# A two-layer hybrid trunk: the mixers normalise probabilities before they are transposed and move them wide over stationary values, and the second mixer's local branch works on chunks of 128 tokens

## The chip, the cores and the metric

The kernel is one program on 1 core of one Trainium2 chip. The metric is the device time in microseconds of that core. It was run 3 times before the change.

## The reference

A trunk of two layers on x of 512 tokens by 1024 channels, in float32. Each layer is a half-weighted SwiGLU, a mixer, and another SwiGLU, each with an RMS norm that is shifted and scaled by a projection of the condition c. Between the two layers one shared set of keys and values for three branches is projected. The mixers are what the change touches:

```python
# first mixer (MoBA): with 512 tokens and blocks of 256 its selection keeps every past block: causal attention
p = jax.nn.softmax(jnp.concatenate([s_own, s_sel], axis=-1), axis=-1)
# second mixer: branches (window, dilation) = (128, 1), (512, 4), (2048, 16), each a band of 128 strided keys or fewer
m = jnp.max(s, axis=-1, keepdims=True)
p = jnp.exp(s - m)
l = jnp.sum(p, axis=-1, keepdims=True)
o = jnp.einsum('nbhqk,nbkhd->nbqhd', (p / l), v_band)
lse = (m + jnp.log(l))[..., 0]
...
w = jax.nn.softmax(jnp.stack(lses, axis=0), axis=0)
o = jnp.einsum('gbsh,gbshd->bshd', w, jnp.stack(outs, axis=0))
return o.reshape(B, S, ATTN_DIM) @ w_o
```

Both mixers have 16 heads of 64 channels. In the second, weighting the branches by the softmax of their lse is the same as one softmax over the keys of all three.

## The kernel before, in words

All activations lie transposed (channels on the 128 partitions, 512 tokens along the free axis). Float32 accuracy comes from splitting: every operand x is held as a rounded high part and a low part of the type float32r, and a product is three matmuls, hi x hi, lo x hi, hi x lo (`three_passes`, lines 344 to 347). ScalarE makes the high part (line 336), VectorE (DVE) the low one (line 340). Weights stream through two slots of 512 KB (`w_dma`, line 326), read once.

The program's order is: four SwiGLU blocks (ffn0 to ffn3) with mixA between the first two, the shared k/v projection (kv) after ffn1, and mixB between ffn2 and ffn3. Each engine has its order written out; semaphores join them. GpSimd (POOL) does only the rotary additions (lines 1456 and 1462), a few low parts and the stores; SyncE (SP) issues all loads.

A mixer (`pe_mixer`, line 670, with `act_mixer`, `dve_mixer`, `pool_mixer` and `sp_mixer` for the other engines) works in 4 groups g of 4 heads. While group g is projected (24 substeps of 6 matmuls of 512 columns, or 12 of 256 for the values of mixA), the attention of group a = g - 1 runs; the last attention group runs beside the output projection. An attention group has 16 steps, one for each head and each tile of 128 queries. In step s TensorE does, in this order:

- `score`: queries stationary, keys moving. In mixA the past keys, 128 to 512 columns. In mixB the tokens lie sorted by their class modulo 4; the local branch scores all 512 keys under a mask, the two dilated ones 128 each, so 768 columns. Each part is a pair of matmuls, keys high and keys low.
- one or two projection substeps (table `SUBSTEPS`, line 98), or parts of the output projection in the last group (`OUT_SUBSTEPS`, lines 119 to 121, steps 1 to 14).
- `transpose_p`: the step before's probabilities, 1 to 4 or 6 transposes of 128x128.
- `weigh_v`: of two steps before; probabilities stationary, high and low, the values of the head moving (2 x 64 columns, high and low), 2 matmuls for each 128 keys.

Between these, DVE takes the masked minimum of the negated scores in one operation (line 1973), ScalarE the exponential with its row sum (line 1796), ScalarE and DVE split the transposed probabilities (lines 1803 and 1996), and DVE adds the two halves of the output, inverts the row sum and scales (`o_scale`, lines 1981 to 1990). After two heads `transpose_o` turns the output's rows into columns.

Rotated queries and keys go to DRAM and come back per head (`load_k`, `load_q`, `load_v`, lines 1655 to 1710): 8 loads of keys and 4 of queries, each to 32 partitions, of 192 KB in mixB and 64 KB in mixA, and one load of values. They have two slots, so a head's loads are held until the head before has begun:

```python
sp.wait_ge(done, (a * 4 + (0 if layer == "A" else HEADS) + j - 1) * 4 + 1)   # head_free, line 1657
```

In mixB the third branch's queries skip DRAM at a group's end (line 1681): read out at step 14 (`READ_OUT`, line 108), added by POOL, split by ScalarE and DVE, then sent on. SP works through its list in order: keys, queries, values, weight units.

Of the kernel before, what the change touches and what calls it, by code (L numbers as in the profile page):

```python
# [32 lines left out]
P = 128  # L33
# [88 lines left out]
OUT_HIGH = {0: 2, 1: 3, 3: 4, 5: 5, 7: 6, 8: 7, 12: 8, 15: 9}  # L122
OUT_LOW = {1: 2, 2: 3, 4: 4, 6: 5, 8: 6, 9: 7, 13: 8}
OUT_ADD = {1: 0, 2: 1, 4: 2, 5: 3, 7: 4, 9: 5, 12: 6}
OUT_IN = {13: (6,)}
POOL_ROWS = (0, 1, 2, 3, 4, 6)


OUT_BY_POOL = 5
OUT_IN_AHEAD = {"mixA": {10: (0,), 11: (1,), 12: (2,), 13: (3,), 14: (4,)}, "mixB": {11: (0, 1), 12: (2, 3), 13: (4,)}}  # L130
TAIL_BANK = {"woA": (0, 1, 2, 3, 4, 6, 5, 0), "woB": (0, 1, 2, 4, 5, 6, 7, 0)}
# [16 lines left out]
def build(nc, x_t, c_col, ada_first, ada, ada_bias, gains, gate_up, down, mixa_w, kv_w, mixb_w, cos_t, sin_t,  # L148
          mask_a, mask_b, ident_in, out):
    with ExitStack() as ctx:  # L150
# [47 lines left out]
        with ExitStack() as mixer_space:  # L198
# [9 lines left out]
            probs = sb(mixer_space, "probs", [P, 2, 6 * P])  # L208
            pt_hi = sb(mixer_space, "pt_hi", [P, 2, 6 * P], F32R)
            pt_lo = sb(mixer_space, "pt_lo", [P, 2, 6 * P], F32R)  # L210
            o_rows = sb(mixer_space, "o_rows", [P, TT, 4 * HD])
            att = sb(mixer_space, "att", [P, KT, S])
            m_a = sb(mixer_space, "m_a", [P, TT * P], BF16)
            m_b = sb(mixer_space, "m_b", [P, TT, 6 * P], BF16)
            negmax = sb(mixer_space, "negmax", [P, 2])
            denom = sb(mixer_space, "denom", [P, 4])
            rdenom = sb(mixer_space, "rdenom", [P, 2])
# [11 lines left out]
        scores = flat[:, 4 * 512:4 * 512 + 6 * P]  # L229
        pt_ps = flat[:, 6 * 512:6 * 512 + 6 * P]  # L230
        O_BANK = {"A": 5, "B": 3}
        OT_BANK = {"A": 7, "B": 3}
        V_BANK = 4

# [40 lines left out]
        q_landed, k_landed, v_landed = sem("q_landed"), sem("k_landed"), sem("v_landed")  # L275
# [3 lines left out]
        s_done, negmax_done, exp_done = sem("s_done"), sem("negmax_done"), sem("exp_done")  # L279
        t_done, pt_hi_done, pt_lo_done = sem("t_done"), sem("pt_hi_done"), sem("pt_lo_done")  # L280
        pv_done, rd_done, o_done = sem("pv_done"), sem("rd_done"), sem("o_done")
        o_sum_done = sem("o_sum_done")
        ot_done = sem("ot_done")
        att_done = sem("att_done")
# [2135 lines left out]
```

## Time and profile before

| what | value |
|---|---|
| median of 3 runs | 2465.88 us (2465.1 to 2468.98) |
| profiled execution, its span | 2469.2 us, within 0.1% of the slowest of the three runs |
| PE busy | 2432.8 us, 99% |
| DVE busy | 1378.1 us, 56% |
| ScalarE busy | 867.2 us, 35% |
| POOL busy | 143.2 us, 6% |
| moved by DMA | 408.8 MB, mean 166 GB/s |

Engine names in the rows: PE is TensorE, PEld its weight loads, DVE VectorE, ACT ScalarE, POOL GpSimd, SPq the DMA issues of SyncE. A line of the timeline gives start, duration, engine, source line, operation, output <- inputs, and in brackets the idle time before it. The duration of a matmul includes its way through the array, and the next one starts before it ends; what one costs is the distance to the next one's start. PEclk is the granted share of TensorE's full clock. The DMA share is the mean busy share of the 16 DMA engines in a stretch. mixA's attention lies between 457 and 680 us, mixB's between 1751 and 2080 us.

### The profile page before, as it was taken

How to read it: one execution, taken by the hardware profiler on the slowest of the kernel's cores; microseconds unless marked ns; L12 is line 12 of the kernel's file. 1: busy time of each engine (PE TensorE's matmuls, PEld its weight loads, DVE VectorE, ACT ScalarE, POOL GpSimd, SP SyncE). 2: the span in 40 equal slices, each digit the busy share in tenths (PEclk: the TensorE clock that was granted, in tenths of full speed). 3: DMA queues.
4: the chain of work that ended last, by engine and by line, in shares of the span. 5: the costliest groups of instructions: out<-in, count | busy, mean ns of one | idle time of the engine just before them, and what ended most of it. 6: DMA issues, size and time to landing. Idle time of an engine off the chain costs nothing. (4 is left out here: it accounts for less than half of the span.)

```text
span 2469.2 us, 33249 instructions
## 1 busy us (share of the span) xinstructions
PE 2432.8 (99%) x11992; PEld 2022.7 (82%) x11997; DVE 1378.1 (56%) x2103; ACT 867.2 (35%) x1233; POOL 143.2 (6%) x130
## 2 busy tenths in 40 slices
PE   9999999999999999999999999999999999999998
PEld 6888888888778888888888888888888887888886
DVE  7555546777675654465545555446667667333333
ACT  3322224445343332233333333223444444333221
POOL 0000000212000000011211000000211100000000
PEclk9999999999999999999999999999999999999999
DMA  6665543665446654336557656436878973222332
GB/s 246 192 194 188 167 126 92 214 192 179 143 154 194 188 181 138 103 114 214 185 189 246 191 182 196 132 119 166 245 218 224 240 214 93 94 93 93 102 94 85
DMA packets 135779, 408.80 MB, mean 166 GB/s; under 512 B 17152, under 2 KB 17536, under 8 KB 135680
## 3 DMA queue, kind: packets, MB, share of 16 engines
q1 hardware_dynamic: 122624, 357.16, 47.8%
q0 software_dynamic: 13056, 50.33, 5.7%
q8 instruction: 60, 0.98, 0.2%
q14 instruction: 39, 0.32, 0.0%
HBM read 353.42 MB, written 52.43 MB: 164 GB/s over the span
## 5 line engine op out<-in xcount | busy, mean ns | idle before, releaser
L340 DVE TENSOR_TENSOR w_lo<-w_raw,w_hi 128x1024 fp32r<-128x1024 f32 (+2 forms) x386 | 473.9, 1228 | 605.4 <-ACT w_hi L336 605.1
L345 PE MATMUL ps<-h_hi,w_hi 128*128 128x512 f32 x1872 | 744.7, 398 | 5.9 <-DVE w_lo L340 2.7
L347 PE MATMUL ps<-h_hi,w_lo 128*128 128x512 f32 x1872 | 731.6, 391 | 0.0
L346 PE MATMUL ps<-h_lo,w_hi 128*128 128x512 f32 x1872 | 730.9, 390 | 0.0
L336 ACT CAST w_hi<-w_raw 128x1024 fp32r<-128x1024 f32 (+2 forms) x388 | 395.6, 1020 | 757.8 <-PE ps L347 737.1
L345 PEld LDWEIGHTS ps<-h_hi,w_hi 128*128 128x128 f32 x1872 | 352.8, 188 | 81.5 <-DVE w_lo L340 5.3
L347 PEld LDWEIGHTS ps<-h_hi,w_lo 128*128 128x128 f32 x1872 | 352.3, 188 | 74.9
L346 PEld LDWEIGHTS ps<-h_lo,w_hi 128*128 128x128 f32 x1872 | 353.0, 189 | 66.9 <-issue 0.2
L345 PE MATMUL ps<-act_hi,w_hi 128*128 128x512 f32 x704 | 275.3, 391 | 0.3 <-DVE w_lo L340 0.2
L347 PE MATMUL ps<-act_hi,w_lo 128*128 128x512 f32 x704 | 274.1, 389 | 0.0
L346 PE MATMUL ps<-act_lo,w_hi 128*128 128x512 f32 x704 | 273.9, 389 | 0.0
L1334 DVE TENSOR_TENSOR prod<-ps,silu_g 128x512 f32<-128x512 f32 x86 | 59.5, 692 | 259.2 <-ACT silu_g L1292 259.2
L892 DVE SCALAR_TENSOR_TENSOR ada_acc<-ada_raw,c_act,ada_acc 128x1024 f32<-128x1024 f32 x126 | 161.2, 1279 | 0.7
L345 PEld LDWEIGHTS ps<-act_hi,w_hi 128*128 128x128 f32 x704 | 132.1, 188 | 31.3 <-issue 4.3
L347 PEld LDWEIGHTS ps<-act_hi,w_lo 128*128 128x128 f32 x704 | 132.1, 188 | 27.9
L346 PEld LDWEIGHTS ps<-act_lo,w_hi 128*128 128x128 f32 x704 | 132.2, 188 | 27.1
L1803 ACT CAST pt_hi<-ps 128x768 fp32r<-128x768 f32 (+4 forms) x128 | 78.4, 612 | 215.4 <-PE ps L754 215.2
L1292 ACT ACTIVATE silu_g<-ps 128x512 f32<-128x512 f32 x86 | 51.5, 599 | 252.3 <-PE ps L347 252.0
L1996 DVE TENSOR_TENSOR pt_lo<-ps,pt_hi 128x768 fp32r<-128x768 f32 (+4 forms) x128 | 92.4, 722 | 80.7 <-ACT pt_hi L1803 79.8
L773 PE MATMUL ps<-v_st,pt_hi 128*128 128x128 f32 x544 | 129.8, 278 | 4.6 <-DVE o_rows L1990 4.6
L774 PE MATMUL ps<-v_st,pt_lo 128*128 128x128 f32 x544 | 128.1, 275 | 0.0
L1456 POOL TENSOR_TENSOR rotated<-tmp 128x512 f32<-128x512 f32 x32 | 43.5, 1359 | 1425.6 <-DVE tmp L1023 1233.4
(162 smaller groups left out, 2802.6 us busy)
## 6 DMA issues: line engine op xcount, KB each, us to landing
w_raw<-gate_up SPq DMA_DIRECT2D x176, 512.0 KB, 3.7
ada_raw<-ada SPq DMA_DIRECT2D x144, 512.0 KB, 4.5
w_raw<-down SPq DMA_DIRECT2D x80, 512.0 KB, 3.6
w_raw<-kv_w SPq DMA_DIRECT2D x48, 512.0 KB, 3.5
w_raw<-mixa_w SPq DMA_DIRECT2D x34, 512.0 KB, 3.9
w_raw<-mixb_w SPq DMA_DIRECT2D x34, 512.0 KB, 5.9
kb<-rot_st POOLq DMA_DIRECT2D x12, 1024.0 KB, 5.0
k_hi<-kb SPq DMA_DIRECT2D x64, 192.0 KB, 5.0
```

The costliest lines, as they stand in the source:

```text
L336: nc.scalar.copy(w_hi[:, slot, 0:n], w_raw[:, slot, 0:n]).then_inc(w_hi_done, 1)
L340: eng.tensor_tensor(w_lo[:, slot, 0:n], w_raw[:, slot, 0:n], w_hi[:, slot, 0:n].bitcast(F32), ALU.subtract).then_inc(w_lo_done[slot], 2)
L345: nc.tensor.matmul(out_ap, l_hi, r_hi, start=start, stop=False, skip_group_check=skip)
L346: nc.tensor.matmul(out_ap, l_hi, r_lo, start=False, stop=False, skip_group_check=skip)
L347: return nc.tensor.matmul(out_ap, l_lo, r_hi, start=False, stop=stop, skip_group_check=skip)
L773: nc.tensor.matmul(o_ps, pt_hi[:, s % 2, cols], v_both, start=n == 0, stop=False)
L774: mm = nc.tensor.matmul(o_ps, pt_lo[:, s % 2, cols], v_both, start=False, stop=n == n_last)
L892: nc.vector.scalar_tensor_tensor(out=ada_acc[:], in0=ada_raw[:, slot, :], scalar=c_act[:, k:k + 1], in1=ada_acc[:], op0=ALU.mult, op1=ALU. ...
L1292: nc.scalar.activation(silu_g[:, b, :], ps[:, 2 * b, :], ACT.Silu).then_inc(silu_done, 1)
L1334: nc.vector.tensor_tensor(prod[:, b, :], ps[:, 2 * b + 1, :], silu_g[:, b, :], ALU.mult).then_inc(pair_free, 1)
L1803: nc.scalar.copy(pt_hi[:, s % 2, 0:w], pt_ps[:, 0:w]).then_inc(pt_hi_done, 1)
L1996: nc.vector.tensor_tensor(pt_lo[:, s % 2, 0:w], pt_ps[:, 0:w], pt_hi[:, s % 2, 0:w].bitcast(F32), ALU.subtract).then_inc(pt_lo_done, 1)
```

## The change

Both mixers: the row sum is inverted right after the exponential, POOL multiplies the probabilities by it, and they are transposed and split already normalised. `weigh_v` now runs once per head: values are stationary (their high half and low half side by side give 128 output rows), the normalised probabilities of up to four query tiles move over them, and the output comes out transposed. `transpose_o` goes; ScalarE copies one half (`fold_copy`), DVE adds the other (`fold_add`). Transposes run 2 steps (mixA) or 5 steps (mixB) behind the scores.

mixB: the local branch takes queries and keys in token order, in chunks of 128, each chunk against itself and the one before: 128 or 256 columns instead of 512. The dilated branches stay sorted by class. So a row of local scores and a row of dilated scores belong to different tokens; minimum and sum are kept per branch kind, exchanged by one small matmul per head (`exchange`, `lanes`), and the joint factor is built by ten small DVE operations and one exponential, once per head, before POOL scales that head's four steps. The rotary additions write the local branch in chunk order. The values of the local branch are loaded by 4 DMAs to 32 partitions each.

```diff
-OUT_SUBSTEPS = {1: [(0, (5,)), (1, (5,))]}
-OUT_SUBSTEPS |= {step: OUT_PARTS[2 * step - 4:2 * step - 2] for step in range(2, 7)}
-OUT_SUBSTEPS |= {step: OUT_PARTS[step + 3:step + 4] for step in range(7, 15)}
+LAG = {"A": 2, "B": 5}
+SLOTS = {"A": 4, "B": 6}
+OUT_SUBSTEPS = {
+    "A": {4: OUT_LAST} | {step: OUT_PARTS[2 * step - 10:2 * step - 8] for step in range(5, 10)}
+    | {step: OUT_PARTS[step:step + 1] for step in range(10, 18)},
+    "B": {7: OUT_LAST} | {step: OUT_PARTS[step - 8:step - 7] for step in range(8, 16)}
+    | {step: OUT_PARTS[2 * step - 24:2 * step - 22] for step in range(16, 21)}}
...
+                if st >= 2:
+                    pe.wait_ge(negmax_done["B"], 2 * st - 2)
+                q, past = q_st[:, sl, 0, tile], slice(max(i - 1, 0) * P, (i + 1) * P)
+                kh, kl = k_hi[:, sl, 0, past], k_lo[:, sl, 0, past]
...
+            def exchange(h):
+                pe.wait_ge(spread_ready, 2 * h + 2)
+                nc.tensor.matmul(spread_ps, lanes[:, 0:P], spread_in[:].rearrange("p s e x y -> p (s e x y)"),
+                                 start=True, stop=True).then_inc(spread_done, 1)
...
+            def weigh_v(h):
...
+                if is_a:
+                    for n in range(TT):
+                        for pt in (pt_hi, pt_lo):
+                            mm = nc.tensor.matmul(o[:, n * P:], v(0, n), pt[:, n, n:4, :].rearrange("p i q -> p (i q)"),
...
+                by_chunk = o.rearrange("p (t c l) -> p t c l", t=4, c=4)
+                for c in range(4):
+                    for b in (1, 2):
+                        for pt in (pt_hi, pt_lo):
+                            nc.tensor.matmul(by_chunk[:, :, c, :], v(b, c),
+                                             pt[:, c, 1 + b, :].rearrange("p (t l) -> p t l", t=4),
...
+            def begin(st, first=(), second=()):
+                if st < ROWS:
+                    score(st)
+                for part in first:
+                    part()
+                if not is_a and st % 4 == 0 and 4 <= st <= ROWS:
+                    exchange(st // 4 - 1)
+                if (st - lag) % 4 == 0 and st - lag >= 4:
+                    weigh_v((st - lag) // 4 - 1)
+                for part in second:
+                    part()
+                if 0 <= st - lag < ROWS:
+                    transpose_p(st - lag)
...
+            for c in range(4):
+                sp.dma_start(v_st[32 * c:32 * c + 32, j % 2, 0].rearrange("p t a d -> p t (a d)").bitcast(F32),
+                             dram_v["B"][a, 0, j].rearrange("(u l) (t n) -> l u t n", l=32, t=4)[:, :, c, :]
+                             ).then_inc(v_landed[j % 2], 16)
...
+                for e, cols in enumerate((slice(P if i == 0 else 0, 2 * P), slice(2 * P, 4 * P))):
+                    op = nc.gpsimd.tensor_scalar(slot[:, cols], slot[:, cols], factor_b[:, h % 2, e, i:i + 1], 1.0,
+                                                 ALU.mult, ALU.mult)
```

Two places where the order of instructions matters. On SP, in a group of mixB with projections, one head's loads (k_hi, k_lo, q_st, v_st are the slots of keys, queries and values; kb, qb, vb the tensors in DRAM; w_raw a weight slot). Before:

```order
L1644 DMA k_hi<-kb 32x3x512 x2
L1644 DMA k_lo<-kb 32x3x512 x2
L1644 DMA k_hi<-kb 32x3x512 x2
L1644 DMA k_lo<-kb 32x3x512 x2
L1644 DMA q_st<-qb 32x3x512 x4
L1672 DMA v_st<-vb 128x3x512
```

and now:

```order
L1678 DMA k_hi<-kb 32x3x512 x2
L1678 DMA k_lo<-kb 32x3x512 x2
L1678 DMA k_hi<-kb 32x3x512 x2
L1678 DMA k_lo<-kb 32x3x512 x2
L1678 DMA q_st<-qb 32x3x512 x4
L1719 DMA v_st<-vb 32x4x128 x4
L1722 DMA v_st<-vb 128x2x512
```

Keys and queries are loaded as before; the values (of the head before that one now) take five DMAs instead of one, four of them of 32 partitions.

On PE, in the last attention group of mixB, one early step that isn't a head's first (probs are the probabilities before the transposes, pt_hi and pt_lo after, ps is the accumulator). Before, step 5:

```order
L744 MATMUL ps<-k_hi,q_st 128x512
L745 MATMUL ps<-k_lo,q_st 128x512
L744 MATMUL ps<-k_hi,q_st 128x128
L745 MATMUL ps<-k_lo,q_st 128x128
L744 MATMUL ps<-k_hi,q_st 128x128
L745 MATMUL ps<-k_lo,q_st 128x128
L345 MATMUL ps<-h_hi,w_hi 128x512
L346 MATMUL ps<-h_lo,w_hi 128x512
L347 MATMUL ps<-h_hi,w_lo 128x512
```

and now the whole step:

```order
L776 MATMUL ps<-k_hi,q_st 128x256
L777 MATMUL ps<-k_lo,q_st 128x256
L780 MATMUL ps<-k_hi,q_st 128x128
L781 MATMUL ps<-k_lo,q_st 128x128
L780 MATMUL ps<-k_hi,q_st 128x128
L781 MATMUL ps<-k_lo,q_st 128x128
L796 MATMUL ps<-ident,probs 128x128 x4
```

The local pair is 256 columns wide, the parts of the output projection behind the score have moved to steps 7 to 20, and the value products stand once per head.

## Rows read from the trace of the kernel before

**Rows 1.** The page: the span, and part 1's first engine.
```profile
span 2469.2 us, 33249 instructions
...
PE 2432.8 (99%) x11992; PEld 2022.7 (82%) x11997; DVE 1378.1 (56%) x2103; ACT 867.2 (35%) x1233; POOL 143.2 (6%) x130
```
**Rows 2.** Windows view: mixB's attention groups two to four.
```profile
core 0: us, PE busy (x) PEld busy (x) DVE busy (x) ACT busy (x) POOL busy (x), PEclk, DMA share, GB/s
...
1828.30:1911.60 83.30, 81.53 (x538) 72.30 (x538) 57.13 (x117) 37.66 (x59) 9.88 (x9) 1.00 0.85 230
1911.60:1993.80 82.20, 80.19 (x531) 71.09 (x530) 55.45 (x117) 38.66 (x63) 16.18 (x14) 1.00 0.88 226
1993.80:2082.70 88.90, 86.39 (x556) 75.53 (x556) 57.62 (x122) 39.59 (x66) 3.67 (x2) 1.00 0.62 166
```
**Rows 3.** Timeline view of PE in mixA: start us, duration us, then the matmul.
```profile
577.37 0.45 PE L744 MATMUL ps<-k_hi,q_st 128*128 128x512 f32 x1
...
577.89 0.39 PE L345 MATMUL ps<-h_hi,w_hi 128*128 128x512 f32 x1
578.11 0.39 PE L346 MATMUL ps<-h_lo,w_hi 128*128 128x512 f32 x1
...
581.14 0.27 PE L773 MATMUL ps<-v_st,pt_hi 128*128 128x128 f32 x1
581.26 0.27 PE L774 MATMUL ps<-v_st,pt_lo 128*128 128x128 f32 x1
...
583.03 0.60 PE L754 MATMUL ps<-ident,probs 128*128 128x128 f32 x4
583.39 0.31 PE L773 MATMUL ps<-v_st,pt_hi 128*128 128x128 f32 x1
...
584.09 0.33 PE L744 MATMUL ps<-k_hi,q_st 128*128 128x256 f32 x1
...
584.38 0.39 PE L345 MATMUL ps<-h_hi,w_hi 128*128 128x512 f32 x1
```
**Rows 4.** Timeline view of SP's DMA issues: first key loads of head 10 in mixB.
```profile
1932.97 1.58 SPq L1644 DMA_DIRECT2D k_hi<-kb  x2
```
**Rows 5.** Tile view of q_st: the same head's query loads, last of its twelve.
```profile
L1644 SPq DMA_DIRECT2D q_st<-qb x4: 317/365/373, 1938.0 to 1939.4; - x4
...
DMA to landing us min/median/max: 5.6/6.1/6.6
```
**Rows 6.** Timeline view of PE: first scores of heads 9 and 10 in mixB.
```profile
1931.69 0.48 PE L744 MATMUL ps<-k_hi,q_st 128*128 128x512 f32 x1 [0.74 <-issue]
...
1948.89 0.45 PE L744 MATMUL ps<-k_hi,q_st 128*128 128x512 f32 x1
```
**Rows 7.** Windows view: a stretch of key and query loads, one of weight and value loads.
```profile
1787.00:1795.00 8.00, 8.00 (x59) 7.31 (x58) 5.35 (x13) 3.89 (x6) 1.06 (x1) 1.00 1.06 219
...
1782.00:1784.50 2.50, 2.50 (x16) 2.11 (x16) 2.39 (x7) 0.63 (x2) 0.00 (x0) 1.00 1.06 419
```
**Rows 8.** Timeline view at a group's end: step 14, read-out, rotation, low part, DMAs, next score.
```profile
1891.90 0.45 PE L744 MATMUL ps<-k_hi,q_st 128*128 128x512 f32 x1
...
1896.72 0.68 DVE L1440 TENSOR_TENSOR tmp<-ps,sin 128x512 f32<-128x512 f32 x1
...
1898.72 1.27 POOL L1462 TENSOR_TENSOR rotated<-tmp 128x512 f32<-128x512 f32 x1
...
1902.52 1.21 DVE L1480 TENSOR_TENSOR rot_st<-rotated,rot_st 128x1024 fp32r<-128x1024 f32 x1
...
1903.76 2.70 SPq L1681 DMA_DIRECT2D q_st<-rot_st  x4
...
1911.57 0.39 PE L744 MATMUL ps<-k_hi,q_st 128*128 128x512 f32 x1
```
**Rows 9.** Windows view at the end of mixA's third group: before and in a clock drop.
```profile
614.00:618.00 4.00, 2.55 (x16) 1.82 (x15) 3.53 (x10) 1.35 (x4) 2.43 (x2) 1.00 0.62 148
618.00:621.40 3.40, 3.40 (x10) 2.62 (x9) 0.35 (x2) 0.00 (x0) 0.00 (x0) 0.50 0.96 345
```

More of the change, by code:

```diff
@@ L1607, in pool_kv @@
             body(0, True)
-            with pool.Fori(1, G * NB // 2) as i:
+            for i in range(1, G * NB // 2):
                 body(i)
@@ L1756, in sp_mixer @@
[L1756 to L1768 removed]
+                        unit(g, 5)
@@ new lines, in sp_mixer, with out_unit, loads @@
+            group = group_a if layer == "A" else group_b
+            group(0, None)
+            for g in range(1, G):
+                group(g, g - 1)
+            a = G - 1
+            def out_unit(n):
+                w_dma(sp, u0 + n, n % 2, weights[n])
+            def loads(j):
+                load_k(sp, layer, a, j)
+                load_q(sp, layer, a, j)
+            if layer == "A":
+                loads(1)
+                load_v(sp, "A", a, 1)
+                loads(2)
+                out_unit(28)
+                out_unit(29)
+                load_v(sp, "A", a, 2)
+                out_unit(30)
+                out_unit(31)
+                loads(3)
+                out_unit(32)
+                load_v(sp, "A", a, 3)
+                out_unit(33)
+                return
@@ new lines, in begin, with add @@
+            def begin(st):
+                if is_a and 1 <= st <= ROWS:
+                    scale(st - 1)
+                if not is_a and st % 4 == 1 and 5 <= st <= ROWS + 1:
+                    for i in range(4):
+                        scale(st - 5 + i)
+            def add(g, pair):
+                n = g * (2 if is_a else 3) + rope0 // 2 + pair
+                first = g == 0
+                rope_add(pool, g * 3 + p0 + pair, n, name if pair == 0 and first else None,
+                         (1 if is_a else 1 + pair) if pair > 0 and first else None, chunks=not is_a and pair == 0)
@@ new lines, in pool_mixer @@
+            for pair in range(3):
+                if not (is_a and pair == 2):
+                    add(0, pair)
+                store(0, pair)
+            if is_a:
+                pool.wait_ge(k_landed, 128)
+                rot_store(pool, rope0 // 2 + 1, dram_q["A"][0, 0], q_stored)
+            adds = {2: 0, 8: 1} if is_a else {2: 0, 8: 1, 14: 2}
+            stores = {5: 0, 11: 1, 15: 2}
+            for g in range(1, G):
+                for s in range(STEPS):
+                    begin((g - 1) * STEPS + s)
+                    if s in adds:
+                        add(g, adds[s])
+                    if g == G - 1:
+                        for k in POOL_IN_AHEAD[name].get(s, ()):
+                            pool_out_in(pool, wo, k)
+                    if s in stores:
+                        store(g, stores[s])
@@ L2146, in build @@
+            for s in range(STEPS + lag + 1):
+                if s == POOL_LAST[layer]:
+                    pool_out_in(pool, wo, POOL_ROWS[-1])
+                begin((G - 1) * STEPS + s)
+            w_split_lo(pool, UNIT0[wo] + 9, 1)
         block = ctx.enter_context(nc.Block())
```

765 lines of the change are left out of this document (404 added, 361 removed).

## The prediction

> **What bounds the kernel now.** I read the page first: TensorE (PE) is busy for 2432.8 of 2469.2 us [rows 1], so time comes out only where PE's own work shrinks, and only as far as nothing else then makes PE wait. The windows view of three attention groups of the second mixer comes next [rows 2]: 83.3, 82.2 and 88.9 us each, PE busy for 97%, VectorE (DVE) for 57 of 83 us, but the 16 DMA engines for 0.85 and 0.88. That last column is what the prediction turns on. The PE timeline [rows 3] gives what a matmul costs, as the distance between starts (the durations overlap): a 512-column one 0.22 (577.89 to 578.11), a 128-column one 0.12 in the printed rows and 0.11 over longer runs of them, a pair of 128 some 0.22, a score pair of 512 columns 0.52, a pair of 256 0.29, four transposes 0.36 to 0.40, 0.10 each. The counts below are the code's.
>
> **PE work, first mixer.** A head's value products are 20 of 128 columns (rows of probabilities stationary); they become 2 each of 512, 384, 256 and 128 (values stationary). 20 x 0.11 = 2.2 us becomes 2 x (0.23 + 0.17 + 0.12 + 0.11) = 1.27; 384 and 256 alone are put between the 128 and the 512 by columns. The 2 transposes of the output per head (0.2) go. 1.15 us less for each of 16 heads: 18.
>
> **PE work, second mixer**, per head. Scores: 4 x (0.52 + 2 x 0.22) = 3.84 becomes, with 128 or 256 local columns, 0.66 + 3 x 0.73 = 2.85. Transposes: 24 become 15, 2.4 to 1.5. Value products: 48 of 128 columns, 5.3, become 18 of 128 and 6 of 256, 2.7. Output transposes: 0.2 go. Added: one matmul of 64 columns in plain f32, which no row has in that width; between a pair of 128 columns (0.22) and one of 512 (0.52) I take 0.25, as it is narrower than the first. 11.8 becomes 7.3, so 4.5 x 16 = 72 us. **PE work falls by 90 us.** The k/v stage only orders rotated columns otherwise on GpSimd, whose cover is the whole stage's matmuls: 0.
>
> **Other engines.** DVE loses the row sum and scaling per step (three short ones) and halves the columns of its largest two; it gains a second minimum, some ten tiny operations and one 512-column add per head. It stays near 58 us of a group, under PE's 66. GpSimd now multiplies every probability: 1920 columns per head. Its two-input operation takes 1.27 us for 512 [rows 8], so 4.7 us per head at most, beside a head window of 13; the lag of five steps holds it. It waits in program order behind its rotations (2.5 us), also inside the lag. I cost both at 0, and they are in the upper part of the range.
>
> **What then waits: the loads of the second mixer.** A head's keys and queries come in 12 DMAs of 192 KB to 32 partitions each, and SyncE may send them only once the first score of the head before has run. Head 10: first score of head 9 at 1931.69 [rows 6], first K load 1932.97 [rows 4], last Q load issued at 1939.4 and landed 6.6 later at most [rows 5], so 14.3 us after that score; head 10's first score ran at 1948.89 [rows 6]. **The slack was 2.9 us of 17.2.** The chain can't shrink: such loads run at 219 GB/s with all 16 engines occupied (share 1.06; packets overlap), where weights run at 419 at the same share [rows 7]; 2.36 MB / 219 = 10.8 us. The change doesn't touch them. It does change the values' load: the local 256 KB now also go to 32 partitions in pieces of 512 bytes. At 219 instead of 419 that is 1.2 instead of 0.6 us; nothing shorter than 2 KB is in this stage, so the upper end is twice that.
> Windows of PE work per head afterwards, in a group with projections (one projection step is 6 x 0.23 = 1.4):
> - heads 0 and 3: 7.3 + 8 x 1.4 = 18.5. Head 0 covers the 14.3 of the next head's loads.
> - heads 1 and 2: 7.3 + 4 x 1.4 = 12.9, with change-overs between kinds 13.3. DMA time per head is 10.8 (keys, queries), 2.5 (values), 1.3 (one weight unit) and 1.9 (three quarters of a 1 MB store at 419) = 16.5. Two heads in a row: the second set of loads lands some 30.7 us after head 1's first score (3 to start, 10.8, 6.1 of the others, 10.8), PE's work is 26.6: 4 us of waiting per group.
> - group end: the queries of the next group go through DVE, GpSimd, ScalarE, DVE and a DMA [rows 8]. Step 14's score, to which the read-outs are tied, stood at 1891.90, the last DMA was issued by 1906.46, and I add 1.2 for its landing (64 KB, nothing in front): 15.8 us. PE's work in that time was 19.7 (next score at 1911.57) and is now step 14 (1.1), step 15 (2.6) and five projection steps (6.9), 10.6. 4.5 to 5 us of waiting at each of 3 group ends.
> - last group: the output-projection parts move from steps 1 to 14 to steps 7 to 20, so steps 0 to 6 hold attention alone. Windows 7.3, 8.7 and 12.9 against 14.3: 7 + 5.6 + 1.5 = 14 us.
> In sum 3 x 8.5 + 14 = 40 us. The first mixer's loads are a third of the size; 12 issues take 6.8 us (1932.97 to 1939.8) [rows 4, 5] and some 2 to land, against 10 or more of PE work in a head, except in the last group, where four steps without parts hold 4 to 5: 4 us.
> **The clock.** PE ran at half clock for 3.4 us (granted 0.50, 1.2 instead of 2.4 GHz) after a stretch of 4 us in which it was busy for 2.55 [rows 9]. Waits of 5 us are such stretches. Where PE is then the bound (three group ends) each costs half of 3.4: 5 us; in the last group the next loads cover it. The Trainium skill (TensorE: Matmul & The Clock Gate, Part 1) has the half clock as the default that activity releases, so it would add as much behind every long wait.
>
> **Sum**: 2469.2 - 90 + 40 + 4 + 5 = 2428 for the profiled span. The median of the runs lies 3.3 below that span: 2425. Ends of the unknown costs: waits of 20 (engines interleave the loads better, the query chain shortens with DVE's load) to 70 (512-byte pieces at the dear end, stores that fall in front of keys, GpSimd late).
>
> **Rivals.**
> - *All waits covered*: PE stays the only bound: 2466 - 90 + 5 to 25 = 2381 to 2401. For it: DMA share was 0.85, not 1. Against: the same DMA time, 0.85 x 83 = 71 us per group, doesn't fit in 83 - 18 = 65. 16%.
> - *DMA bound with gaps*: a group can't run under 71 + 3 for the values, plus idle DMA time whenever SyncE stands at a semaphore (now a tenth of the group): 80 us per group, so the second mixer gains only in its last group; with clock losses 2445 to 2460. 16%.
> - *The column order costs the matmuls*: 16 of a head's 24 value products write four runs of 32 columns each, spread over a whole bank. All 128-column rows here write one run. If a write of the bank's full spread costs as a 512-column one, 0.23 instead of 0.11, 256 x 0.12 = 30 us come back: 2455, 4%. **It decides the sign** from 0.11 + 41/256 = 0.27 us each; at 0.45 (double a 512-column one) it adds 87, 2512: slower. The Trainium skill (SBUF — State Buffer, Door 1, its note on cache lines) says that any non-contiguous access to PSUM slows matmuls much. For it: the rule names no shortest run; against: runs of 32 f32 are contiguous over far more than one such line. 5%.
> - That the change doesn't do what it says I rule out by the order of its instructions: the counts above are read there.
>
> **Chances.** Forecast (waits of 30 to 65 us, 2405 to 2445) 58%; covered 16%; DMA bound 16%; column order, part 4%, slower 5%; all cancelled, 1%. 0.2% (5 us) is what a measurement of this kernel tells from no change. Faster 0.93, same 0.02, slower 0.05. The range leaves out half of the covered case and the slower one: 2393 to 2455.
>
> **What would show it.** PE busy down by about 90 us and its idle time up by 35 to 50, nearly all of it before the first score of a head and ended by the landing of keys or queries; group periods near 68, 74, 73 and 85 us; DMA share in the groups at 0.95 or more; more stretches of granted clock 0.5. Wrong if value products stand further apart than 0.12, if PE waits mainly for scaled probabilities (GpSimd) or for DVE, or if the DMA share stays under 0.9 while PE still waits.

## The result and the profile after

| | median of the runs | ratio to before, 95% interval |
|---|---|---|
| before | 2467.1 us (4 runs, beside those of the change) | |
| after | 2505.9 us (2503.8 to 2512.6, 4 runs) | 1.0161, 1.0146 to 1.0176 |

Slower by 39 us where 41 us faster was forecast. The profiled execution, whose span of 2510.8 us is used below, is the longest of the four; the spans of the others are 2502.0 to 2505.2. The page of the changed kernel, its span, the engines and, in 40 slices, the granted clock of TensorE (PE):

```profile
span 2510.8 us, 31515 instructions
...
PE 2393.7 (95%) x11245; PEld 1972.4 (79%) x11245; DVE 1325.9 (53%) x2087; ACT 875.2 (35%) x1397; POOL 250.1 (10%) x322
...
PEclk9999999999899999999999999999999879999999
```

Against [rows 1] PE is busy 39 us less, not 90, although the products forecast away are away. It also stands idle for 117 us, not 36. The windows view cuts the two mixers into their first three attention groups and the rest (last group up to the norm behind it). Before:

```profile
core 0: us, PE busy (x) PEld busy (x) DVE busy (x) ACT busy (x) POOL busy (x), PEclk, DMA share, GB/s
457.60:624.80 167.20, 161.67 (x1039) 142.69 (x1040) 116.85 (x342) 79.79 (x184) 30.78 (x27) 0.99 0.63 199
624.80:692.30 67.50, 63.03 (x340) 49.96 (x339) 46.76 (x129) 31.08 (x70) 3.90 (x2) 1.00 0.36 112
1751.00:1993.80 242.80, 237.50 (x1578) 211.03 (x1579) 166.93 (x347) 113.85 (x181) 36.73 (x33) 1.00 0.84 224
1993.80:2087.20 93.40, 89.98 (x571) 76.97 (x570) 61.97 (x129) 42.41 (x70) 3.67 (x2) 1.00 0.59 158
```

After, the same four stretches:

```profile
456.90:628.30 171.40, 151.35 (x856) 127.58 (x857) 95.62 (x254) 83.99 (x187) 65.12 (x74) 0.97 0.63 192
628.30:713.10 84.80, 68.49 (x299) 52.69 (x297) 44.83 (x105) 36.56 (x76) 13.09 (x19) 0.88 0.32 94
1770.20:2010.70 240.50, 197.36 (x1115) 167.86 (x1113) 140.83 (x403) 107.73 (x287) 79.85 (x120) 0.91 0.88 223
2010.70:2128.80 118.10, 98.48 (x509) 83.49 (x509) 59.24 (x169) 46.78 (x117) 23.40 (x43) 0.83 0.55 132
```

Three things stand in these rows. The loss lies in the two last groups: 67.5 to 84.8 us and 93.4 to 118.1, together +42. The three groups with projections are 4.2 longer in mixA and 2.3 shorter in mixB, though PE's work there fell by some 63 us (the table below). And the clock, 0.99 to 1.00 before, is 0.97, 0.88, 0.91 and 0.83.

To part these I took every distance between two matmul starts of both traces. The lower quartile of a kind of pair at full clock is its **work**; of what a distance has above it, the part inside a stretch of granted clock 0.5, up to once the work, is **half clock**, the rest **waits**:

| us | length | work | half clock | waits |
|---|---|---|---|---|
| mixA, groups 1 to 3 | 167.2 to 171.4 | 149.6 to 140.1 | 1.6 to 4.7 | 16.9 to 27.2 |
| mixA, last group | 67.5 to 84.8 | 58.9 to 57.4 | 0 to 7.9 | 9.0 to 19.6 |
| mixB, groups 1 to 3 | 242.8 to 240.5 | 225.1 to 171.3 | 0 to 17.1 | 18.6 to 53.6 |
| mixB, last group | 93.4 to 118.1 | 85.4 to 80.4 | 0 to 16.9 | 8.5 to 21.3 |
| change | +44 | -70 | +45 | +69 |

The three parts of a row add up to its length within 1.5 us. They depend on which pairs count as one kind: told apart by tiles and widths alone, single entries move by up to 5 us and the sums read -68, +44 and +68. Outside the mixers the changed kernel is 2 us shorter. **Waits and half clock give back 114 us for 70.** The waits view of PE names the waits in mixB (us in total, times, longest; DVE is VectorE, and pt_lo the low part of the split transposed probabilities):

```profile
PE ps L776 <- DMA q_st<-rot_st: 13.7, 3, 4.8
PE ps L821 <- DVE pt_lo L2123: 11.4, 9, 3.0
PE ps L796 <- DVE pt_lo L2123: 10.8, 12, 1.4
PE ps L787 <- DVE spread_in L2088: 8.8, 7, 2.4
PE ps L776 <- issue: 8.6, 5, 3.3
```

L776 are a head's first scores, L821 value products, L796 transposes, L787 the exchange. The first and the last row (22 us) stand before a head's first scores, where the forecast had put its waits for queries and keys; the trace names no releaser for the last, and run 11 shows that it was the loads. The three between (31 us, all ended by DVE) were not forecast. In mixA:

```profile
PE ps L812 <- DVE pt_lo L2123: 10.8, 11, 2.8
PE ps L796 <- DVE pt_lo L2123: 10.3, 16, 1.9
PE ps L765 <- DVE negmax L2062: 5.9, 14, 1.3
```

Before, the largest such row in either mixer was 3.2 us. Now one exchange and what follows, from the timeline (start us, duration us):

```profile
1896.06 1.22 DVE L1513 TENSOR_TENSOR rot_st<-rotated,rot_st 128x1024 fp32r<-128x1024 f32 x1
1897.19 0.28 DVE L2062 CUSTOM_DVE_ANT_0 probs<-ps,m_b 128x128 f32<-128x128 f32 x1
...
1897.75 0.29 DVE L2088 TENSOR_TENSOR spread_in<-stats,lanes 128x32 f32<-128x32 f32 x2
...
1898.09 0.43 PE L787 MATMUL ps<-spread_in,lanes 128*128 128x64 f32 x2 [1.78 <-DVE spread_in L2088]
...
1899.76 0.73 PE L377 MATMUL ps<-h_hi,w_hi 128*128 128x512 f32 x1
1900.20 0.69 DVE L2123 TENSOR_TENSOR pt_lo<-ps,pt_hi 128x512 fp32r<-128x512 f32 x1 [0.75 <-ACT pt_hi L1903]
1900.29 0.63 PE L378 MATMUL ps<-h_lo,w_hi 128*128 128x512 f32 x1
1900.71 0.63 PE L379 MATMUL ps<-h_hi,w_lo 128*128 128x512 f32 x1
...
1901.51 3.54 POOL L2259 TENSOR_SCALAR probs<-probs,factor_b 128x128 f32<-128x128 f32 x8 [2.84 <-DVE factor_b L2115]
...
1902.42 0.26 PE L821 MATMUL ps<-pt_hi,v_st 128*128 128x128 f32 x1
...
1905.13 0.52 PE L796 MATMUL ps<-ident,probs 128*128 128x128 f32 x3
```

DVE's queue has a rotation's split of 1.2 us ahead of what the exchange needs; PE stands 1.78 us at L787. The transposes that PE began at 1898.36 were split by 1900.89, 2.5 us later; in between ScalarE had stood 0.97 us for the exchange's result before it could round them. Behind it the projection matmuls are 0.42 to 0.53 apart in place of 0.23: the clock fell at 1899.1, for 3.4 us. The 24 value products take 1902.42 to 1905.13, 2.7 us, as forecast.

The clock also stays low in stretches where PE doesn't wait. Windows of the last group of mixB, steps 0 to 6, in which no output part stands:

```profile
2010.70:2016.00 5.30, 3.70 (x19) 3.38 (x19) 2.51 (x13) 1.67 (x6) 0.81 (x1) 0.60 0.68 219
2016.00:2021.00 5.00, 5.00 (x24) 5.00 (x25) 1.03 (x6) 1.09 (x4) 3.54 (x8) 0.50 1.05 243
...
2027.00:2033.00 6.00, 4.46 (x19) 4.12 (x20) 3.27 (x14) 2.28 (x9) 0.00 (x0) 0.50 0.83 206
2033.00:2039.00 6.00, 6.00 (x29) 6.00 (x30) 1.18 (x6) 1.83 (x6) 3.54 (x8) 0.50 1.03 226
```

### The profile page after: what moved, and what is told of

It is laid out like the page before. It is cut to its first block and busy times, and to the rows that moved or that the text cites. A ratio compares the mean times of both kernels' runs of the same rounds, so it can differ in the third digit from the quotient of the medians.

```text
span 2510.8 us, 31515 instructions
## 1 busy us (share of the span) xinstructions
PE 2393.7 (95%) x11245; PEld 1972.4 (79%) x11245; DVE 1325.9 (53%) x2087; ACT 875.2 (35%) x1397; POOL 250.1 (10%) x322
## 5 line engine op out<-in xcount | busy, mean ns | idle before, releaser
L377 PE MATMUL ps<-h_hi,w_hi 128*128 128x512 f32 x1872 | 749.5, 400 | 18.9 <-DVE w_lo L372 6.2
L377 PEld LDWEIGHTS ps<-h_hi,w_hi 128*128 128x128 f32 x1872 | 356.9, 191 | 95.1 <-DVE w_lo L372 11.1
L377 PE MATMUL ps<-act_hi,w_hi 128*128 128x512 f32 x704 | 275.3, 391 | 0.0
L377 PEld LDWEIGHTS ps<-act_hi,w_hi 128*128 128x128 f32 x704 | 132.1, 188 | 31.0 <-issue 3.9
L2123 DVE TENSOR_TENSOR pt_lo<-ps,pt_hi 128x512 fp32r<-128x512 f32 (+3 forms) x128 | 73.2, 572 | 129.7 <-ACT pt_hi L1903 128.4
L1888 ACT ACTIVATE probs<-probs,stats 128x256 f32<-128x256 f32 (+1 forms) x128 | 62.4, 488 | 116.0 <-DVE stats L2062 115.9
L796 PE MATMUL ps<-ident,probs 128*128 128x128 f32 x400 | 71.5, 293 | 21.0 <-DVE pt_lo L2123 21.0
```

The costliest lines, as they stand in the source:

```text
L377: nc.tensor.matmul(out_ap, l_hi, r_hi, start=start, stop=False, skip_group_check=skip)
L796: mm = nc.tensor.transpose(pt_ps[:, n, :], probs[:, st % SLOTS[layer], n * P:(n + 1) * P], ident[:])
L1888: nc.scalar.activation(slot[:, cols], slot[:, cols], ACT.Exp, bias=stats[:, h % 2, 0, e, i:i + 1], scale=-1.0, accum_out=stats[:, h % 2, 1 ...
L2123: nc.vector.tensor_tensor(lo, src, hi.bitcast(F32), ALU.subtract).then_inc(pt_lo_done[layer], 1)
```

## The experiments

In the order in which they ran; the kernel before was run beside each set of them (medians 2466.2 to 2469.1). The changed kernel, 2505.9, is the reference unless another is named.

**1. Fillers before known waits.**
```diff
+ nc.tensor.matmul(ps[:, 3, 64:], idle[:, 0:P], idle[:, 64:], start=True, stop=True)
+ FILL_HEAD, FILL_SPREAD, FILL_WEIGH = (14, 2, 5, 0), (1, 1, 6, 1), (3, 2, 0, 3)   # how many, by h % 4
```


> Some 150 matmuls on a tile of zeros (0.2 us each at full clock, 29 us in all) stand in the second mixer where the trace of the changed kernel shows TensorE waiting: ahead of the first scores of a head, of the exchange and of the value products. Their results are never read. Theory C (the waits are what drops the clock to 0.5, and the half clock costs by itself some 32 us in this mixer beside the waits): the granted clock there rises from 0.73-0.92 to 0.97 or more, the fillers lie inside waits, and the kernel is 15 to 25 us faster than the changed kernel, 2481 to 2491. Rival L (the waits are latency and transfers; at full clock TensorE would only wait longer for them): the clock rises too, the time stays within 5 us of 2506. Rival W (the fillers are work like any other): 2520 to 2535.

2511.8 us (1.0169, 1.0148 to 1.0189). In mixB waits fell by 14 us, work rose by 15, half clock went from 34 to 31. Theory C fell: zeros ahead of the waits did not bring the clock back, and the time came out a little above what rival L allows. Whether waits alone set the clock is left open by this.

**2. Loads one step earlier.**
```diff
-  if h >= (1 if layer == "A" else 2): sp.wait_ge(s_done[layer], 4 * (h - 1) + 1)
+  if h >= 2: sp.wait_ge(s_done[layer], 4 * (h - 1))     # k_landed, q_landed: one semaphore per slot
```


> The keys and queries of a head are sent for when the last scores of the head two before are done, not one step later, after the first scores of the head before (the landings are counted on two semaphores in turn, for the order). Theory L (TensorE's waits before the first scores of a head, 24 us in the second mixer, are the transfer's, and it starts a step too late): the waits for the second to fourth heads of a group (some 10 us) go, those at a group's start (4.7 us each, the query chain) stay, a few clock drops go with them: 2490 to 2500. Rival D (DMA queues full, share 0.85 to 0.94 there: sent earlier, not landed earlier): 2503 to 2508.

2506.9 us (1.0155, 1.0134 to 1.0177): level. Rival D's result: the waits of 8.6 us before other heads' first scores read 8.3.

**3. The exchange at its step's end** (PE, ACT and DVE alike).
```diff
+  if 0 <= st - lag < ROWS: transpose_p(st - lag)     # DVE: split_pt, then find_gap and joint_factor
   if not is_a and st % 4 == 0 and 4 <= st <= ROWS: exchange(st // 4 - 1)
-  if 0 <= st - lag < ROWS: transpose_p(st - lag)
```


> Second mixer: the exchange across the groups of 32 partitions and what DVE and ACT do with it stand at the end of their step, behind the transposes, their rounding and their splitting. Theory X (TensorE waits 7 us for the exchange's operand and DVE, standing in the exchange, holds up the split that the value products one step on wait for, 11 us): 8 to 15 us faster than the changed kernel, 2491 to 2498. Rival F (the factors then come late and the transposes of the next step wait for POOL's scaled rows instead): 2500 to 2515, with a new row of TensorE waiting for scaled probabilities.

2493.9 us (1.0100, 1.0083 to 1.0117): 12 us of the 39 by the medians (14 when each is set against the runs of the kernel before beside it), as theory X had it, and the largest single gain of the study. The waits of PE in mixB now:

```profile
PE ps L796 <- DVE pt_lo L2123: 17.9, 16, 2.0
PE ps L776 <- DMA q_st<-rot_st: 12.2, 3, 4.7
PE ps L776 <- issue: 11.3, 7, 2.5
...
PE ps L787 <- DVE spread_in L2088: 2.7, 5, 1.2
...
PE ps L821 <- DVE pt_lo L2123: 0.7, 1, 0.7
```

The exchange went from 8.8 to 2.7 and the value products from 11.4 to 0.7, but the transposes from 10.8 to 17.9: a part of the repaired wait opened one step on.

**4. No scaling by POOL.**
```diff
-  pe.wait_ge(scaled_done[layer], st + 1)
+  pe.wait_ge(exp_done[layer], st + 1 if is_a else 2 * st + 2)
```


> Both mixers: POOL scales nothing, and the transposes wait for the exponentials alone; the probabilities go on unscaled (this part of the computation is left out). Theory N (normalising first puts factor and scaling into the chain, and the lags of 2 and 5 steps don't cover it): 15 to 30 us faster, 2476 to 2491, and the waits of TensorE for pt_lo fall by half. Rival S (the scaling is covered by the lags; the waits are the turn of the one PSUM bank of the transposes through ACT and DVE): 2500 to 2506, waits as they were.

2505.6 us (1.0148, 1.0130 to 1.0165). POOL's busy time fell from 250 to 146 us and the time stayed: rival S. PE's waits for pt_lo in mixB read 8.8 and 10.8 us, for 11.4 and 10.8. As it stands the change doesn't lose by the scaling.

**5. Projection parts ahead of a group's first scores** (on run 3).
```diff
-  pre = FIRST_PRE[layer] if g == 1 else PRE
+  pre = FIRST_PRE[layer] if g == 1 or not is_a else PRE        # 10 in place of 6; SUBSTEPS likewise
```


> On top of the late exchange (2493.9): in the second mixer four gemm parts (1.4 us each) move from the first four steps of a group ahead of the group's first scores, where TensorE waits 4.7 us for the landing of the last query block. Theory Q (that wait is latency, and work put there is free; the steps they leave get short, but not shorter than the 14.3 us in which the next head's keys and queries come): the three waits of 4.7 us go, with them the clock drop behind each: 12 to 20 us faster than 2493.9, 2474 to 2482. Rival M (the parts are missing in the first head: its steps wait for the landing of the second head and for the turn of the transposes' bank instead): 2490 to 2500.

2491.6 us (1.0094, 1.0078 to 1.0111): within the noise of run 3. Two of three waits for the query block went, and a new one of 3.8 us each took their place (`PE ps L377 <- DVE tmp L1468: 7.6, 2, 3.8`, the read-out of the bank of a later part). Rival M's time by another wait than it named.

**6. A part for step 14 of mixA** (on run 3).
```diff
+  steps = {step: steps.get(step, ())[:1] if step == 3 else steps.get(step, ()) for step in range(4)} \
+      | {step: (step + 9,) for step in range(4, 15)}
```


> On top of the late exchange: in the first mixer the gemm parts of steps 3 to 13 are shifted by one, so that step 14, which had none, has one (step 3 has one in place of two). Theory G (the value products of step 14 wait 1.6 to 2.3 us for the split just before them because no part lies between): these three waits and the two clock drops behind them go, 5 to 9 us faster than 2493.9. Rival H (every part taken out of one step opens the same wait in another): 2491 to 2497.

2516.6 us (1.0197, 1.0180 to 1.0214), 23 us slower than run 3, which neither theory had. The first three groups of mixA became 190.7 us in place of 170.7, and the value products of nine of their twelve heads now waited 2.2 to 3.2 us for pt_lo. PE's table was shifted and those of ACT and DVE (weight splits, read-outs) were not. That their queues then stand at a part that comes a step later, with the split of the probabilities behind it, fits; it was not tried with all tables shifted.

**7. Two banks for mixA's transposes** (on run 3).
```diff
+  def pt_bank(layer, st): return ps[:, 7 if layer == "A" and st % 2 == 1 else 6, :]
-  return ps[:, 5 if layer == "B" or h % 2 == 0 else 7, :]
+  return ps[:, 5, :]
```


> On top of the late exchange: in the first mixer the transposes take banks 6 and 7 in turn and the value products one bank in place of two, so that transposes wait for the split of the tile two back. Theory B (TensorE waits 10 us there for the turn of the one bank): these waits fall below 3 us, with them a clock drop or two: 8 to 14 us faster than 2493.9, 2480 to 2486. Rival P (ACT's rounding and DVE's splitting are simply late, the next reader waits for them instead: the value products and the scores): 2489 to 2496.

2491.2 us (1.0094, 1.0077 to 1.0111). Waits of mixA 46.6 to 46.1: rival P. The waits of the transposes for the split (9.6 us in run 3) went, and those of the scores for DVE's minimum grew from 5.5 to 14.1: the bank's turn was the name of the wait, not its cause.

**8. Fillers in the last group's bare steps** (on run 3).
```diff
+  if not is_a and 3 * STEPS <= st < 3 * STEPS + 7: fill(pe, 6, (st - 1) // 4)
```


> On top of the late exchange: at the end of steps 0 to 6 of the last group of the second mixer, which have no gemm part, six matmuls on zeros, 448 columns wide, each 0.19 us at full clock (8 us in all), their results never read. In the changed kernel the clock stood at 0.5 for 24 of some 32 us there, though TensorE waited only 5 us. Theory N (a stretch of nothing but 128-column products, transposes and short waits is what drops the clock): the clock goes to 0.9 or more there and gives back more than the fillers take: 2484 to 2492. Rival I (the clock answers to idle time, and there is nothing to fill): still 0.5, 2502 to 2512.

2490.8 us (1.0098, 1.0081 to 1.0114); the profiled span was 6.6 us under run 3's, the medians differ by 3, which is not separable. In mixB's last group half clock fell from 12.6 to 6.9 us while work rose by 5.6. The first 32 us of that group, in run 3 and with the fillers:

```profile
2001.00:2033.00 32.00, 26.64 (x129) 24.99 (x130) 14.54 (x57) 12.84 (x40) 7.90 (x17) 0.63 0.95 224
1993.10:2025.10 32.00, 28.57 (x184) 23.08 (x184) 15.76 (x61) 15.11 (x46) 7.89 (x17) 0.91 0.97 229
```

The granted clock rose from 0.63 to 0.91, as theory N had it, but the fillers cost about what they buy. In run 1, whose fillers stood ahead of waits, the same stretch kept 0.62.

**9 to 12. Five repairs together, a longer lag in mixA, thin loads, all of it.**
```diff
  # e9: runs 3, 2 and 7, step 0's two parts ahead of mixB's scores, and in mixA
+ parts = {0: [(1, (0, 1))], 1: [(1, (2, 3))], 2: [(0, (4,))], 3: [(1, (4,))]} if is_a else {}
  # e10, on run 3; the last group's tables for A one step later
- LAG = {"A": 2, "B": 5}
+ LAG = {"A": 3, "B": 5}
  # e11, on the changed kernel
+ to = 64 if n_b == NB and 4 * a + j >= 2 else S      # tokens per load of keys and queries
```


> Five small repairs at once: the late exchange, the earlier loads of keys and queries, two banks for the first mixer's transposes, the two gemm parts of step 0 of a second-mixer group ahead of its first scores, and the four output parts that the first mixer crowds into step 15 spread over steps 0 to 3 of its last group, which had none. Theory A (the losses are many short waits, each with its own cause, and each repair takes its own away, with the half-clock stretches behind it): 2470 to 2480, still not under the kernel before. Rival O (a repaired wait opens in the next step, since each step is shorter than the round trip through ACT and DVE): 2484 to 2492.

> On top of the late exchange: in the first mixer the transposes follow the scores by three steps in place of two, so that the value products come in steps 3, 7, 11 and 15, and the tables of the last group's output parts are one step later. Theory G2 (the first mixer loses because a head's value products meet its last split with too little between): the waits for the split of 1.6 to 2.9 us in step 14 go: 5 to 9 us faster than 2493.9. Rival E (the last group ends a step later and its steps without gemm parts are one more): 2492 to 2500.

> The changed kernel, but from the third head of the second mixer on each load of keys and queries carries 64 of 512 tokens, with as many transfers and semaphores (the scores of these heads use stale rows: this part of the computation is left out). Theory T (the waits of some 10 us before the scores of heads inside the groups are the transfers' size): these go, the query chain at a group's start stays, 8 to 16 us faster than 2505.9, 2490 to 2498. Rival I (what is waited for is the issue and the latency of twelve transfers, not their size): 2500 to 2507. An upper bound for what any better order of loads can give.

> The five repairs together with the lag of three steps in the first mixer. Theory A with G2: 2465 to 2474, level with the kernel before. Rival O: within 3 us of the five repairs without it.

Run 9 gave 2486.9 us (1.0083, 1.0066 to 1.0100), 7 better than run 3 by the medians and 4 by the ratios: rival O. In the profiled executions 6 us of it lie in mixA. There four output parts, two of them half ones (4 us of work), had moved from the end of the third group into the bare steps of the last; the third group became 4.0 us shorter (59.6 to 55.6) and the last only 1.2 longer (86.3 to 87.5). Run 10 gave 2490.0 (1.0101, 1.0085 to 1.0118), between the ranges of its two theories and level with run 3 by the ratio; run 12 gave 2492.7 (1.0097, 1.0072 to 1.0122), 6 over run 9, where one theory had it much faster and the other within 3: a longer lag alone doesn't mend mixA. Run 11, 2503.7 (1.0149, 1.0131 to 1.0167), answers the prediction's main mechanism. The second and third groups of mixB, of the changed kernel, then with thin loads:

```profile
1840.10:1922.30 82.20, 69.61 (x405) 59.26 (x405) 48.92 (x141) 36.76 (x97) 26.16 (x41) 0.92 0.94 231
1922.30:2010.70 88.40, 71.93 (x399) 61.28 (x399) 50.19 (x141) 38.10 (x101) 32.12 (x46) 0.90 0.85 214
```
```profile
1840.30:1921.20 80.90, 67.76 (x405) 57.26 (x405) 49.59 (x141) 36.78 (x97) 26.20 (x41) 0.94 0.49 141
1921.20:2009.70 88.50, 71.85 (x399) 61.36 (x399) 50.19 (x141) 38.12 (x101) 32.16 (x46) 0.90 0.45 128
```

The DMA share halves, 0.94 and 0.85 to 0.49 and 0.45, and the periods stay within 1.3 us. That is rival I's time, but not its mechanism. PE's waits in mixB now:

```profile
PE ps L821 <- DVE pt_lo L2124: 13.1, 9, 3.0
PE ps L787 <- DVE spread_in L2089: 12.5, 10, 2.4
PE ps L796 <- DVE pt_lo L2124: 10.6, 12, 1.4
...
PE ps L776 <- issue: 1.9, 1, 1.9
```

The waits before other heads' first scores went from 8.6 to 1.9 us, as theory T had it, so the size of the loads did hold them. But the three rows that DVE ends rose from 31.0 to 36.2, and the time fell by 2 us only, within the noise. The query chain's 13.7 us stayed.

**13 to 16. The value products spread again.** After twelve runs 20 us had no shown cause, and a new theory stood: the products used to fill every step.
```diff
-  for c in range(4): ...
-  for n in range(TT): ...
+  for c in ((0, 1), (2,), (3,))[piece]: ...      # dilated branches; pieces 2, 3 and 4 steps behind the head's first transposes
+  for n in ((0,), (1,), (2, 3))[piece]: ...      # local branch
   # e16, on run 14; steps 0 to 6 of the last group
+  fill(pe, 4, (st - 1) // 4)
```


> On top of the late exchange (2493.9): in the second mixer the 24 value products of a head, the same ones, stand in three of four steps (10, 6 and 8, each piece as soon as its tiles are split) in place of one. Theory R (the gathered products leave three steps of four shorter than the round trip of the transposes through ACT and DVE): TensorE's waits for the split, 18 us, fall by half or more, and half-clock stretches with them: 8 to 15 us faster, 2479 to 2486. Rival K (the steps' length was never the limit, or a product piece meets a split that has only just been asked for): 2490 to 2500.

> The five repairs (2486.9) with the products spread as well. Theory R: 2473 to 2480. Rival K: 2484 to 2492.

> The repairs but for the first mixer's two banks, the products of the second mixer spread as in the run before, and those of the first mixer in two pieces (tiles 0 and 1, then 2 and 3; 12 products in place of 8, as many columns). Theory R for the first mixer too (its value products wait 1.6 to 2.9 us for the last split with all eight behind it): 3 to 8 us faster than the run with the second mixer's alone, 2468 to 2476. Rival K: level with it, or slower by 1 to 3 us for the four more products per head.

> The second kernel of this call with four 448-column matmuls on zeros at the end of steps 0 to 6 of the second mixer's last group (28 of 0.19 us, 5.3 us in all). Theory N (narrow work alone drops the clock, some 24 us at 0.5 in that stretch, 10 us lost by it): net 2 to 6 us faster than without them. Rival: the fillers cost what they give, within 2 us.

2497.9 (1.0122, 1.0105 to 1.0139), 2488.9 (1.0088, 1.0071 to 1.0105), 2491.1 (1.0106, 1.0083 to 1.0128) and 2482.4 us (1.0065, 1.0049 to 1.0082). Theory R fell three times, and rival K's time came each time. In run 13 the waits for the split barely moved, 18.6 us before, 17.1 now, and another name appeared above them:

```profile
PE ps L796 <- POOL probs L2264: 14.4, 14, 1.7
PE ps L796 <- DVE pt_lo L2128: 10.5, 9, 2.4
PE ps L824 <- DVE pt_lo L2128: 6.6, 8, 1.4
```

Run 16 is 6.5 us under run 14, with 28 matmuls more. The intervals of the ratios just overlap, but the two ran in one set, and the four times of each don't overlap (2482.0 to 2483.7, and 2485.6 to 2490.6). The first 32 us of mixB's last group had a granted clock of 0.56 in run 14 and of 0.89 in run 16, and the group went from 114.0 to 108.0 us: the one place where fillers pay. It is the fastest form of the change, and still 16 us behind the kernel before.

**17 and 18. Is it the scaling now?** Both on run 16.
```diff
  # e18; the last group's tables for B one step later
- LAG, SLOTS = {"A": 2, "B": 5}, {"A": 4, "B": 6}
+ LAG, SLOTS = {"A": 2, "B": 6}, {"A": 4, "B": 7}
```


> On top of the fastest so far (2482.4, all repairs, products spread, fillers in the last group): POOL scales nothing and the transposes wait for the exponentials alone (the normalisation is left out). Theory F (once the other waits are short, a head's first transposes wait for the joint factor and POOL's eight scalings, 15 us in the second mixer): these waits go and 8 to 15 us with them, 2467 to 2475, where the same edit of the changed kernel gave nothing. Rival S2 (the split is behind it at once, as in the first trial): 2479 to 2484.

> On top of the same kernel, correct in full: the second mixer's transposes follow the scores by six steps in place of five, with seven buffers of probabilities (one mask table for both mixers and a quarter of the zero tile make room), and the last group's tables one step later. Theory F: the waits for scaled probabilities go, 5 to 10 us faster, 2472 to 2478. Rival E (one more step at the end, which has few parts to fill it, takes it back): 2480 to 2486.

2484.6 (1.0058, 1.0041 to 1.0075) and 2499.3 us (1.0121, 1.0104 to 1.0138). Theory F fell too: run 17 is level with run 16, and run 18 is some 15 us slower, which neither of its theories had. PE's waits of run 16, then of run 17 without the scaling:

```profile
PE ps L804 <- POOL probs L2280: 14.9, 13, 1.7
PE ps L804 <- DVE pt_lo L2144: 11.1, 9, 2.4
```
```profile
PE ps L804 <- DVE pt_lo L2144: 33.6, 13, 6.2
```

The 15 us on POOL became 22 more on DVE. Run 18 shows where a lag is paid. The first three groups of mixB and the last, in run 16 and in run 18:

```profile
1764.60:1990.10 225.50, 194.67 (x1124) 165.75 (x1122) 136.69 (x403) 108.16 (x287) 79.92 (x120) 0.93 0.93 238
1990.10:2098.10 108.00, 93.11 (x526) 75.94 (x526) 59.65 (x169) 47.34 (x117) 24.25 (x43) 0.94 0.57 144
```
```profile
1766.00:1995.30 229.30, 193.40 (x1110) 165.17 (x1109) 133.64 (x403) 107.04 (x286) 81.70 (x120) 0.92 0.88 234
1995.30:2114.50 119.20, 99.92 (x540) 82.05 (x540) 60.26 (x170) 47.71 (x118) 23.59 (x43) 0.89 0.50 130
```

One more step of lag (with tables that follow it), 3.8 us more in three groups, **11.2 more in the last**, which then has one bare step more at its start and one drain step more at its end; the run doesn't part the two. In mixA the same move didn't lengthen the last group (82.2 us in run 10, 86.3 in run 3). In run 16 the three groups of mixB stand 17 us under the kernel before (225.5 to 242.8) and those of mixA 3 under (163.8 to 167.2); the last groups stand 15 (108.0 to 93.4) and 19 over (86.1 to 67.5). What the change still loses in run 16 stands in the last groups.

## Why the prediction was wrong, step by step

- **PE work, -90.** The prices held: 24 value products of mixB 2.7 us, as forecast, those of mixA 1.33 (533.63 to 534.96) for 1.27. The reckoning finds -70; of the 20 that lack, 9 are waits around the exchange so regular that it counts them as work (its work in mixB falls by another 9 in run 3). The page's busy time fell by 39 only, since a matmul at half clock is busy for longer.
- **Other engines, 0.** This is the step that failed first. I compared sums: DVE 58 of 66 us in a group, POOL 4.7 us a head under a window of 13. DVE was indeed less busy (166.93 to 140.83 us in the first three groups of mixB), and POOL took 3.5 us a head. But of PE's new waits 31 us in mixB and 27 in mixA are ended by DVE, and the prediction itself had named waits mainly for DVE as a sign that it is wrong. Run 3 shows what a sum of busy times can't: the same operations in another order in the queues of PE, ScalarE and DVE took 12 us off. So what held PE there was the place of its next operand in those queues, not how long they work. That PE's steps (the shortest 2.1 to 2.5 us, for 2.5 from a transpose to its split) are simply too short for this round trip fits the rest, but is not shown: theory R, built on it, fell.
- **Waits, +44.** +69 came. The forecast part is in the trace: three waits at the group ends (13.7 for 13.5), and 8.6 before other heads' first scores, for 26. The 13.7 is partly luck: from step 14's score to the next group's first the chain took 16.8 to 16.9 us, not 15.8 (1.2 for a landing had no row), and PE's cover was 12.1, not 10.6. The mechanism of the 8.6, the loads' size, held (run 11), at a third of the forecast. The 69 are more because of the waits that DVE ends.
- **Last group, +14 in mixB, +4 in mixA.** I noted that parts move from steps 1 to 14 to steps 7 to 20 and priced the bare steps by the loads alone. The last groups took 25 and 17 us more. Not priced: the drain behind step 15 (five steps of transposes, splits and products with their chain exposed) and the clock in the bare steps. The clock's share is measured (half clock of 16.9 and 7.9 us); what the drain costs by itself is not.
- **The clock, +5.** 45 came: the term furthest off in proportion. I had taken one drop from the trace of before [rows 9] and one per long wait. Twenty came in the mixers, 116 us at half clock, each with a wait of PE close ahead of it, some as short as 1.1 us; the longest, of 13.7 us, came in mixB's last group in the steps without parts. There the projection and the products behind a wait cost up to twice, for 3.4 us and more each time.
- Work 20 short, waits 25 and half clock 40 over, less 2 outside the mixers, are the 83 us between the forecast span of 2428 and 2510.8. By the medians it is 81 (2425 and 2505.9).
- **The rivals.** The column order cost nothing: 0.111 us apart at four runs of 32 columns, as at one run. The Trainium skill (SBUF — State Buffer, Door 1) has any non-contiguous access to PSUM slow matmuls; for runs of 128 bytes no row here shows it. The slower outcome had 5%, tied to that rule; the mechanism that made it slower, waits ended by DVE with a clock that falls, wasn't among the rivals at all. *DMA bound with gaps* had 80 us per group, and the second and third took 82.2 and 88.4; but with half the DMA share they took 80.9 and 88.5, so its mechanism isn't the one. The forecast's own test, group periods of 68, 74, 73 us, read 69.9, 82.2, 88.4.

What stays open: whether a shared cause, and which, lies under the waits of mixB that moved from name to name in runs 3, 5, 13 and 17. No run took other work (rotations' and weights' splits) out of DVE's queue ahead of the splits that PE waits for. Second groups took 77.2 to 78.3 us in runs 9, 14, 16, 17 and 18, at a DMA share of 0.92 to 0.95; thin loads were only tried on the changed kernel, whose second group took 82.2, so that DMA bounds the repaired ones isn't excluded. Nor was mixB's last group rearranged so that parts stand in its first steps, as run 9 did in mixA.

## What to carry to other kernels

Work that is taken off the bounding engine was also the cover of what the other engines do in between: before counting it as gain, look at what stands ahead of the next operand in each engine's queue, not only at busy sums. Here moving one exchange behind the splits gave back 12 us while no engine's work changed. Price the last group by itself, its bare first steps and its drain: here of the 44 us that the mixers lost, 42 lie there. A wait that is taken away may come back under another name (runs 3, 7, 11 and 17), so go by the time. And where many short waits appear on TensorE, read the granted clock: here its half speed cost 45 us beside 69 of waits.

## What the runs showed of the hardware

- Granted clock 0.5 (1.2 GHz) came in mixB each time with a wait of 1.2 to 4.8 us close ahead, lasted 3.4 to 13.7 us, and was there with PE busy for 5.00 of 5.00 us in value products of 128 and 256 columns. The Trainium skill (TensorE: Matmul & The Clock Gate, Part 1) has the half clock as the default that activity releases; in those 5 us it was not released.
- Matmuls on zeros, 448 columns wide, ahead of waits (run 1) hardly moved it: 0.62 in the first 32 us of mixB's last group, as without them. At the end of steps that had no projection parts they raised it from 0.63 to 0.91 (run 8 to run 3) and from 0.56 to 0.89 (run 16 to run 14).
- A 64-column plain f32 matmul stands as two records; with nothing to wait for, the next matmul starts 0.27 us later (1898.09 to 1898.36), where I had put 0.25.
- POOL multiplies 1920 columns by a scalar column, in eight operations, in 3.54 us.
- Matmuls that write four runs of 32 f32 columns spread over a bank started 0.11 us apart (1902.52 to 1904.08), as those that write one run of 128.
